# In-projection split in 392 and 256 columns, with four low parts on GpSimd and two high parts in later attention pairs

## The reference

```python
h = x @ w_in                                  # 1024 x 648
c_q, k, v, k_idx, w_idx = split(h, [256, 384, 512, 640])
c_q = rms_norm(c_q, g_cq)
q = c_q @ w_uq;  q_idx = c_q @ w_iq
k_idx = layer_norm(k_idx, g_ik, b_ik)
...                                           # rotate, index scores, top 64, attention
out @ w_o
...
q, f, i, g = split(x @ hgrn_w_in, 4)          # recurrence; then rms_norm, gate
o @ hgrn_w_o
```

## Time and profile before

| | |
|---|---|
| median of 3 runs | 949.01 us (948.93 to 949.58) |
| profiled execution | 951.03 us, its span 949.0 us |
| TensorE busy | 923.1 us (97%) |
| VectorE busy | 590.3 us (62%) |
| ScalarE busy | 457.8 us (48%) |
| GpSimd busy | 156.0 us (16%) |
| mean granted TensorE clock | 0.994 |
| chain that ended last, by engine | PE 84%, DVE 8%, ACT 4% |

### The profile page before, as it was taken

How to read it: one execution, slowest core, us unless ns; L and a number is a source line. 1 busy time by engine, 2 the same in 40 slices (tenths; PEclk the granted TensorE clock), 3 DMA queues, 4 the chain that set the end, 5 groups by cost and what they waited for, 6 DMA issues and landing times.

```text
span 949.0 us, 13816 instructions
## 1 busy us (share of the span) xinstructions
PE 923.1 (97%) x5667; PEld 760.8 (80%) x5667; DVE 590.3 (62%) x957; ACT 457.8 (48%) x609; POOL 156.0 (16%) x128
## 2 busy tenths in 40 slices
PE   8989999999999999899999999999999999999996
PEld 6867788888887997688888888878777788888885
DVE  5874774554648579978736456494223567777775
ACT  5775352433433443543425343345656465564653
POOL 3283300000005500013000000040355201010011
PEclk9999999999999999999999999999999999999999
DMA  8981466555646644245755555449432465555531
GB/s 292 208 163 46 148 228 198 179 179 192 204 143 217 221 147 166 92 131 178 245 178 179 192 199 185 164 158 320 133 134 89 155 207 185 185 178 178 180 130 45
DMA packets 104382, 164.98 MB, mean 174 GB/s; under 512 B 4011, under 2 KB 74714, under 8 KB 104320
## 3 DMA queue, kind: packets, MB, share of 16 engines
q1 hardware_dynamic: 101056, 152.61, 48.6%
q0 software_dynamic: 3264, 11.49, 5.6%
HBM read 159.89 MB, written 4.19 MB: 173 GB/s over the span
## 4 chain that ended last, share of the span: by engine, by line
PE 84%; DVE 8%; ACT 4%; DMA 1%; issue 1%; POOL 1%; SPq 0%; DVEq 0%; POOLq 0%; ACTq 0%
PE PG L1791 12%; PE PA L1791 12%; PE PG L1793 12%; PE PG L1792 12%; PE PA L1793 12%; PE PA L1792 11%; DVE wlo L600 1%; DVE work L1516 1%; ACT whi L591 1%; PE PG L1927 1%; PE TB L2379 1%; PE TB L2042 1%; PE TB L1947 1%; PE PA L2196 1%; PE PA L2195 1%
## 5 line engine op out<-in xcount | busy, mean ns | idle before, releaser
L600 DVE TENSOR_TENSOR wlo<-raw,whi 128x2048 fp32r<-128x2048 f32 (+1 forms) x124 | 288.9, 2346 | 65.5 <-ACT whi L591 65.4
L591 ACT ACTIVATE whi<-raw 128x2048 fp32r<-128x2048 f32 (+1 forms) x142 | 268.7, 1908 | 49.9 <-PE PA L1793 18.7
L1791 PE MATMUL PG<-whi,xlo 128*128 128x512 f32 x548 | 218.4, 399 | 0.3 <-DVE xlo L1098 0.2
L1793 PE MATMUL PG<-whi,xhi 128*128 128x512 f32 x548 | 214.1, 391 | 0.0
L1792 PE MATMUL PG<-wlo,xhi 128*128 128x512 f32 x548 | 213.9, 390 | 0.0
L1793 PEld LDWEIGHTS PG<-whi,xhi 128*128 128x128 f32 x548 | 103.1, 188 | 22.0
L1791 PEld LDWEIGHTS PG<-whi,xlo 128*128 128x128 f32 x548 | 103.2, 188 | 21.8 <-DVE wlo L1322 0.8
L1792 PEld LDWEIGHTS PG<-wlo,xhi 128*128 128x128 f32 x548 | 103.3, 189 | 20.1
L1791 PE MATMUL PA<-whi,xlo 128*128 128x512 f32 (+1 forms) x292 | 117.1, 401 | 1.8 <-DVE xlo L1098 1.3
L1793 PE MATMUL PA<-whi,xhi 128*128 128x512 f32 (+1 forms) x292 | 112.5, 385 | 0.0
L1792 PE MATMUL PA<-wlo,xhi 128*128 128x512 f32 (+1 forms) x292 | 112.2, 384 | 0.0
(11 more groups left out here) (289 smaller groups left out, 1175.3 us busy)
## 6 DMA issues: line engine op xcount, KB each, us to landing
raw<-in_ffn_w_gate SPq DMA_DIRECT2D x44, 512.0 KB, 4.0
raw<-in_ffn_w_up SPq DMA_DIRECT2D x44, 512.0 KB, 5.0
raw<-in_ffn_w_down SPq DMA_DIRECT2D x22, 1024.0 KB, 4.8
raw<-in_w_up SPq DMA_DIRECT2D x44, 512.0 KB, 4.6
raw<-in_hgrn_w_in SPq DMA_DIRECT2D x16, 1024.0 KB, 5.3
raw<-in_w_qkv SPq DMA_DIRECT2D x12, 1024.0 KB, 5.3
raw<-in_w_down SPq DMA_DIRECT2D x11, 1024.0 KB, 4.8
raw<-in_att_w_o SPq DMA_DIRECT2D x4, 1024.0 KB, 5.8
```

Of the source, the lines that this page charges most:

```text
L591: nc.scalar.activation(whi[:, g, 0:n_], raw[:, s, 0:n_], ACT.Copy).then_inc(S("w_hi"), 1)
L600: nc.vector.tensor_tensor(wlo[:, s, 0:n_], raw[:, s, 0:n_], whi[:, g, 0:n_].bitcast(F32), ALU.subtract).then_inc(S("w_lo"), 1)
L1791: mm(dst, xl[:, k, rows], whi[:, g, cols], start=first, stop=False)
L1793: return mm(dst, xh[:, k, rows], whi[:, g, cols], start=False, stop=last_)
```

## The change

The first go now has columns 0 to 255 and 512 to 647, 392 in all (`FIRST`); unit 2 has columns 256 to 511, a full unit. The first pieces are 784 columns wide, each by two DMAs of rows of 1024 and 544 bytes. The places in `pin` change with it. On ScalarE, unit 3's high part and the sine move behind the squares, unit 4's behind the turned queries. On VectorE, unit 2's low part moves behind the angles, unit 3's and the queries' low parts stand behind the normalised queries and ahead of the keys' normalisation. GpSimd makes the low parts of units U_H+13 to U_H+16, after its preparation of masks. `hi(7)` moves from after pair 0 to after pair 2, `hi(8)` from after pair 1 to after pair 4.

```diff
-SKIP, EARLY = 392, 256
-C_V, C_KI, C_WI, C_K = 248, 376, 504, 512
+EARLY, SKIP = 256, 512
+FIRST = EARLY + IN_COLS - SKIP
+C_KI, C_WI, C_K, C_V = 256, 384, 392, 520
...
-    a = [[v[:, 4 * j:4 * j + 4, c:c + EARLY] for c in (0, SKIP)] for j in range(2)]
+    a = [[(0, v[:, 4 * j:4 * j + 4, 0:EARLY]), (EARLY, v[:, 4 * j:4 * j + 4, SKIP:IN_COLS])] for j in range(2)]
     a.append([(0, 8, SKIP - EARLY, v[:, :, EARLY:SKIP])])
...
+            for u in range(U_H + 13, U_H + 17):
+                lo_unit(u)
             for b in range(4):
                 power(C_HEADS + b)
...
         def unit_len(u):
-            return 8 * (IN_COLS - 512) if u == 2 else UNIT
+            return 4 * FIRST if u < 2 else UNIT
...
             x_hi_rows("x", 1)
             hi(2)
-            hi(3)
-
-            act.wait_ge(S("ang"), 1)
-            ac.activation(trig.rearrange("p a b c -> p (a b c)"), ang.rearrange("p a b c -> p (a b c)"),
-                          ACT.Sin).then_inc(S("trig"), 1)
             full(1)
-            ac.activation(pin[:, :, 0:512], PG[:, :, :], ACT.Copy).then_inc(S("pin"), 1)
+            ac.activation(pin[:, :, 0:FIRST], PG[:, :, 0:FIRST], ACT.Copy).then_inc(S("pin"), 1)
...
-            hi(4)
+            hi(3)
+            act.wait_ge(S("ang"), 1)
+            ac.activation(trig.rearrange("p a b c -> p (a b c)"), ang.rearrange("p a b c -> p (a b c)"),
+                          ACT.Sin).then_inc(S("trig"), 1)
             turned(ev["cq"])
             ac.activation(flat(xhi[:, 0:2, :]), TB[:, ev["cq"] % 2, :], ACT.Copy).then_inc(S("x_hi"), 1)
-            act.wait_ge(S("cqn"), 1)
+            hi(4)
             full(2)
...
-                if p < 2:
-                    hi(U_AO + 2 + p)
+                if p in (2, 4):
+                    hi(U_AO + 1 + p // 2)
...
             x_lo_rows("x", 1)
-            lo(2)
...
-            lo(3)
-
+            lo(2)
             vec.wait_ge(S("pin"), 1)
...
             ins.then_inc(S("cqn"), 1)
+            lo(3)
+            lo_of_bank(flat(xlo[:, 0:2, :]), ev["cq"], flat(xhi[:, 0:2, :]))
...
-            lo_of_bank(flat(xlo[:, 0:2, :]), ev["cq"], flat(xhi[:, 0:2, :]))
             vec.wait_ge(S("trig"), 1)
...
-            lo(U_H + 13)
             decayed(0)
             take(0)
-            lo(U_H + 14)
             decayed(1)
             take(1)
-            lo(U_H + 15)
             decayed(2)
             take(2)
-            lo(U_H + 16)
             decayed(3)
...
             take(3)
...
+            vec.wait_ge(S("w_lo"), U_H + 17)
             lo(U_H + 17)
...
-                            last = products(bank(r), k, r, u + s, slice(t * 512, (t + 1) * 512), k == 0, k == KT - 1)
+                            n_ = 512 if u else FIRST
+                            last = products(bank(r)[:, 0:n_], k, r, u + s, slice(t * n_, (t + 1) * n_), k == 0, k == KT - 1)
...
-                        last = products(PA[:, 2 + r, 0:136], k, r, U_IN + 2, slice(k * 136, (k + 1) * 136), k == 0,
+                        last = products(PA[:, 2 + r, 0:256], k, r, U_IN + 2, slice(k * 256, (k + 1) * 256), k == 0,
```

More of the change, by code:

```diff
@@ L407, in _ @@
                 for g, landed_ in enumerate((f"first_loaded{u}", f"w_loaded{u}")):
-                    dst = raw[:, u, g * UNIT // 2:(g + 1) * UNIT // 2].rearrange("p (t s c) -> p t s c", s=2, c=EARLY)
-                    for s, view in enumerate(units[u]):
-                        sp.dma_start(dst[:, :, s, :], view[:, 2 * g:2 * g + 2, :]).then_inc(S(landed_), 16)
+                    dst = raw[:, u, g * 2 * FIRST:(g + 1) * 2 * FIRST].rearrange("p (t c) -> p t c", t=2)
+                    for o, view in units[u]:
+                        sp.dma_start(dst[:, :, o:o + view.shape[2]], view[:, 2 * g:2 * g + 2, :]).then_inc(S(landed_), 16)
             sp.dma_start(h[:, 1, :], hv[:, 1, :]).then_inc(S("x_loaded1"), 16)
@@ L758, in _ @@
             x_hi_rows("x", 0)
-            first, second = slice(0, UNIT // 2), slice(UNIT // 2, UNIT)
+            first, second = slice(0, 2 * FIRST), slice(2 * FIRST, 4 * FIRST)
             for u in range(2):
@@ L766, in _ @@
             hi(2)
+            full(1)
+            ac.activation(pin[:, :, 0:FIRST], PG[:, :, 0:FIRST], ACT.Copy).then_inc(S("pin"), 1)
+            act.wait_ge(S("pin"), 1)
+            for r in range(RT):
+                ac.activation(sq[:, r, :], pin[:, r, 0:NQL], ACT.Square,
+                              accum_out=ve[:, 8 + r:9 + r]).then_inc(S("ssq"), 1)
             hi(3)
@@ L771, in _ @@
                           ACT.Sin).then_inc(S("trig"), 1)
-            full(1)
-            ac.activation(pin[:, :, 0:512], PG[:, :, :], ACT.Copy).then_inc(S("pin"), 1)
[L774 to L777, removed]
-            hi(4)
             turned(ev["cq"])
             ac.activation(flat(xhi[:, 0:2, :]), TB[:, ev["cq"] % 2, :], ACT.Copy).then_inc(S("x_hi"), 1)
-            act.wait_ge(S("cqn"), 1)
+            hi(4)
             full(2)
             ac.activation(pin[:, :, C_K:C_K + P], PA[:, 2:4, 0:P], ACT.Copy).then_inc(S("k_in"), 1)
-            ac.activation(pin[:, :, C_V:EARLY], PA[:, 2:4, P:SKIP - EARLY], ACT.Copy).then_inc(S("k_in"), 1)
+            ac.activation(pin[:, :, C_V:C_V + P], PA[:, 2:4, P:SKIP - EARLY], ACT.Copy).then_inc(S("k_in"), 1)
             hi(5)
@@ L1318, in _ @@
             for u in range(2):
-                for part, made, done in ((slice(0, UNIT // 2), "first_hi", "first_lo"),
-                                         (slice(UNIT // 2, UNIT), "w_hi", "w_lo")):
+                for part, made, done in ((slice(0, 2 * FIRST), "first_hi", "first_lo"),
+                                         (slice(2 * FIRST, 4 * FIRST), "w_hi", "w_lo")):
                     vec.wait_ge(S(made), u + 1)
```

## The result

The changed kernel takes 954.44 us (median of 7 runs, 953.21 to 956.69), the kernel before on the same chip 949.58 (7 runs, 948.93 to 951.06): ratio 1.0049 [1.0037, 1.0061], slower by 4.9 us. Forecast were 950.4 and a range up to 953.5, so the time lies 0.9 us above the range. The profiled execution of after is a middle one, 954.44 with a span of 952.5 us.

What follows compares the result with a forecast made beforehand. TensorE was taken to bound the first projection, VectorE the recurrent stage. Front -1.7, high parts -0.15 and low parts +3.25 sum to +1.4 us on the median of 949.01: 950.4, range 942.8 to 953.5.

Steps and rivals of the forecast that it cites:

- Part 3, the exclusion: Recurrent stage: GpSimd's low parts and VectorE's decay products exclude each other for whole instructions, GpSimd holding 4.5 us at a time.
- Rivals 1 to 3: Recurrent stage: VectorE keeps its turn, 947.1 (20%); exclusion doesn't bite, 942.8 (14%); predicated copies excluded too, 956.4 (8%).
- Part 3, the term +3.25: Recurrent stage, four low parts to GpSimd: 12.1 us of new waits less 8.8 saved on VectorE, +3.25 us.
- I take 0 for a second such fall: Recurrent stage: another fall of TensorE's clock behind its gaps costs 0, VectorE being behind it; at most +1.7 us.
- my steps: Recurrent stage, stepped through with exclusion: copies of the four levels end at 374.5, 382.1, 386.7 and 394.7 us.
- Part 1, the front: First and second projection, split in 392 and 256 columns: indexer's queries start at 28.2 instead of 29.9, gain 1.7 us.
- Part 2: Attention, high parts of units 7 and 8 made later: wait at head 5 goes, small ones come, gain 0.15 us.
- Rival 4: Front gives nothing because unit 2's load or the constants come 2 us later than worked out: 952.1, 6%.

Runs made afterwards that it cites:

- experiment 4: After with the four low parts back on VectorE and seven unread matmuls of 512 columns ahead of TensorE's wait for the constants: 950.88 us, ratio 1.0009.
- experiment 7: After with low parts 13 to 16 back on VectorE and GpSimd issuing the constants' six DMAs ahead of the gains' three: 947.86 us, ratio 0.9981.
- low_only: Before with only the low parts of units U_H+13 to U_H+16 moved to GpSimd: 954.23 us, ratio 1.0048.
- low_memset: Before with low parts 13 to 16 taken from VectorE, GpSimd filling each with zeros instead of subtracting: 947.37 us, ratio 0.9980.
- high_only: Before with only the high parts of units 7 and 8 moved to behind pairs 2 and 4: 949.66 us, ratio 0.9999.
- low_placed: Before with low parts 13 to 15 on GpSimd in halves, held back to start beside VectorE's masked copies, 16 on VectorE: 948.12 us, ratio 0.9988.
- low_quarters: Before with low parts 13 to 16 on GpSimd as in the change, each in four subtractions of 128x512: 954.06 us, ratio 1.0043.
- experiment 2: Before with only the split in 392 and 256 columns and the new ScalarE and VectorE orders there: 950.36 us, ratio 1.0006.

## Why the prediction was wrong, point by point

**Part 3, the exclusion: right.** That each engine holds the other for whole instructions, that GpSimd gets in at the border between two queued products, one product of about 5 us and two more blocked, and masked copies undisturbed: all seen. Rivals 1 to 3 are out: VectorE does not keep its turn (365.10), the exclusion bites, and no copy is longer. The rule of the Trainium skill ("GPSIMD Engine Reference", Key points) on which instructions of VectorE contend agrees with these rows: 5.08 us for a product with two operands in SBUF, 3.26, against 3.27 before, for a copy out of PSUM.

**Part 3, the term +3.25: mis-sized, +4.4.** The step that failed is "I take 0 for a second such fall". After the first held product TensorE waits 3.15 us, and then its clock is at the lower level for 3.4 us (granted 0.80 from 373 to 374, 0.50 from 374 to 377). Timeline of TensorE, a window, and the timeline of ScalarE in after:

```profile
372.15 2.39 PE L2245 MATMUL PA<-work 128*32 128x16 f32 x128 [3.15 <-DVE work L1516]
```

```profile
374.00:378.00 4.00, 4.00 (x42) 3.31 (x43) 4.00 (x3) 0.00 (x0) 2.56 (x1) 0.62 0.02 4
```

```profile
383.57 1.92 ACT L594 ACTIVATE whi<-raw 128x2048 fp32r<-128x2048 f32 x1 [11.71 <-PE TB L1790]
```

VectorE was behind TensorE there, but ScalarE's high part of unit 16 was not: it waits for TensorE. Counted from the diagonal it starts at 25.8 us, where I had 25.1; low part 16 with it, 0.8 late, and the copies of the fourth level end 36.9 us after the diagonal instead of 36.0. The copies of the three levels before agree with my steps within 0.2 us. That is 0.9 of the missing 1.1 us. The rest: I had these copies 3.5 us later than before and the cross product only 3.25, while after takes the same 10.3 us from the one to the other as before. What I asked of the slow clock was only whether the bound engine is TensorE, and not who else is fed by it. That the delay of 0.7 us comes from the slow matmuls is read from the order of the rows; no run kept the clock up in this stage with the whole low parts on GpSimd. The prediction did allow +1.7 for a second fall and 0 for the front; both together are 953.8, which its range, to 953.5, left out.

**Part 1, the front: the failed step is the gap costed at its length.** The price of a matmul was right: 0.178 us for 392 columns where I had 0.177, 0.12 for 256 at full clock. That the first projection ends at 19.8 as forecast is in part luck: it began 0.44 us earlier, at 9.87, and took 9.9 us where I had 9.5. The prediction itself had TensorE wait 1.1 us for the constants and then start the second projection at full speed. In after the constants are 0.5 later than worked out and, decisive, the clock falls behind the gap of 1.5 us: of the 2.3 us between 28.2 and 30.52, experiment 4 gives 1.3 back with the clock kept up, and experiment 7 the rest, with the constants early. I had priced a slow clock behind TensorE's gap of 1.75 us in another stage and did not ask the same of a gap that the change makes. The low part of unit 2 ran from 18.75 to 21.04, as foreseen.

**What the front was compared with.** The other half of the error is in the page of before. Executions with the old front reach the diagonal at 356.8 and 356.9 us with full clock at 54 us (`low_only`, `low_memset`) and at 358.1 to 359.1 with the fall there (before, `high_only`, `low_placed`, `low_quarters`). By that the fall costs 1.3 to 2.2 us; counted from the indexer's first product, which takes out how late the first projection began, the diagonal comes 327.1 us later without the fall and 328.8 to 328.9 with it, so 1.7. That most runs of before go without it is read from their times; only one execution of before is profiled. None of the seven profiled executions with the new front has it. So the front of after (diagonal at 357.78) is 1.0 us earlier than the profiled before and 0.9 later than an ordinary one, and the ordinary one sets the median. Setting the sum against a profiled time two microseconds above the median should have made me look for what was rare in it. Whether the new front keeps the clock up at 54 us, or seven executions had luck, is open.

**Part 2: right** in mechanism (the wait of 1.03 us goes, waits of 0.42 and 0.34 come where 0.6 and 0.5 were worked out). Its size, -0.1 against -0.15, is too small for these runs to tell from nothing.

**The sum by medians:** front +0.6 (experiment 2), high parts -0.1, low parts +4.5 (experiment 1), together +5.0, measured +4.9. That it closes this well is luck: the intervals of the three are 1.5 us or so to either side for the front and the low parts and 0.9 for the high parts. Forecast were -1.7, -0.15 and +3.25. Rival 4, the front that gives nothing, was the true case with 952.1, for a reason I had not put there (the clock, not a load of 2 us later), and at 6% far too low; with the larger term of part 3 it becomes 953.2. What is left is that before took 949.58 beside after where the sum had 949.01, and the 0.6 by which the front's median lies above nothing, which its interval (-1.0 to +2.1) does not tell from nothing.

## What to carry to other kernels

Give GpSimd work that reads two operands from SBUF only beside instructions of VectorE that don't read two operands from SBUF, with a count that lets each piece start together with VectorE's copies out of PSUM; smaller pieces without it changed nothing here. Price a gap that a change opens on TensorE by its length and by the slow clock behind it, ask which engine is fed by the slow matmuls, and take the gap away at its source (here the order of nine small DMAs) rather than fill it. Where the profiled execution is not at the median, find what it has that the median lacks before any difference is set against it.

## What was not expected of the hardware

A GpSimd subtraction that waits behind VectorE's product goes first at each border, again and again: with four pieces of 128x512 four products in a row are held, 1.42 to 1.78 us each where they take 0.68. GpSimd's memset of 128x2048 (1.81 us) holds nothing. TensorE stood still for 1.96 and 2.23 us in two kernels, and for 0.34 to 0.79 us at five more places, with no wait in its program, each time until 2.2 to 2.5 us after a packet of instructions began to arrive. Fourteen instructions added 355 us earlier moved these places by seven matmuls: 90 of 128 to go instead of 83.
